# Weight splits one piece further ahead, in rings of five and four, in a two-layer encoder trunk

## The reference

```
h = rms_norm(x); proj = h @ w_in
gates, mla_in, dil_in, diff_in = split(proj)
o_mla  = latent attention (8 heads; q, k, v from normed latents @ w_uq, w_ukv; rope)
o_dil  = 3 dilated windows x 6 heads, mixed by their log-sum-exp; rope
o_diff = softmax(q1 k1) - lam softmax(q2 k2), 4 heads, rms_norm; rope
merged = g_mla*(o_mla @ w_branch_mla) + g_dil*(o_dil @ w_branch_dil) + g_diff*(o_diff @ w_branch_diff)
x = x + rms_norm(merged @ w_out)
h = rms_norm(x); u = conv3(h @ w_up); x = x + rms_norm((gelu(gate) * val) @ w_down)
```

## Time and profile before

| | us |
|---|---|
| median of 3 runs | 1046.75 (1046.65 to 1047.1) |
| the profiled execution | 1046.71 |
| its span | 1044.8 |
| TensorE busy | 1025.7 |
| VectorE busy | 656.4 |
| ScalarE busy | 586.6 |
| GpSimd busy | 121.7 |

### The profile page before, as it was taken

One profiled execution on the slowest core, in us unless ns is written; L12 is line 12 of the kernel. 1 busy time (PEld: TensorE's weight loads), 2 busy tenths in 40 slices (PEclk: granted clock), 3 DMA queues, 4 the chain that ended last, 5 costly groups with the idle time before them and its releaser, 6 DMA issues.

```text
span 1044.8 us, 15963 instructions
## 1 busy us (share of the span) xinstructions
PE 1025.7 (98%) x6332; PEld 918.9 (88%) x6332; DVE 656.4 (63%) x866; ACT 586.6 (56%) x843; POOL 121.7 (12%) x233
## 2 busy tenths in 40 slices
PE   8999999999999999999999999999999999999997
PEld 7889999888877999999898899998888789999996
DVE  5636556654585776776665355656556767676775
ACT  5666666556446645454475666565553466545453
POOL 3353114000000000000024321230000000000000
PEclk9999999999999999999999999999999999999999
DMA  8555445444453554546355544464445435554541
GB/s 253 178 180 158 128 128 190 142 143 161 142 190 112 202 201 162 203 160 220 103 191 163 165 129 124 149 201 161 138 148 178 163 139 179 185 201 163 201 161 41
DMA packets 106221, 170.79 MB, mean 163 GB/s; under 512 B 3377, under 2 KB 72804, under 8 KB 106148
## 3 DMA queue, kind: packets, MB, share of 16 engines
q1 hardware_dynamic: 104860, 166.88, 48.5%
q10 hardware_dynamic: 1208, 2.63, 0.7%
q0 software_dynamic: 80, 0.26, 0.1%
HBM read 168.72 MB, written 1.05 MB: 162 GB/s over the span
## 4 chain that ended last, share of the span: by engine, by line
PE 90%; DVE 4%; ACT 2%; DVEq 2%; issue 1%; POOL 0%; POOLq 0%; ACTq 0%
PE bank L1276 26%; PE bank L1278 26%; PE bank L1277 26%; PE bank L1566 2%; PE bank L1473 1%; PE bank L1494 1%; DVEq L1133 1%; PE bank L1559 1%; DVE merged L1134 1%; DVE hT_lo L1003 1%; PE bank L1482 1%; PE bank L1510 1%; PE bank L1255 1%; PE bank L1517 1%; PE bank L1556 1%
## 5 line engine op out<-in xcount | busy, mean ns | idle before, releaser
L982 DVE TENSOR_TENSOR w_lo<-w_raw,w_hi 128x2048 fp32r<-128x2048 f32 (+3 forms) x174 | 362.9, 2098 | 186.1 <-ACT w_hi L650 186.0
L650 ACT ACTIVATE w_hi<-w_raw 128x2048 fp32r<-128x2048 f32 (+3 forms) x174 | 302.4, 1752 | 49.8 <-PE bank L1278 49.2
L1276 PE MATMUL bank<-w_hi,hT_lo 128*128 128x512 f32 (+2 forms) x700 | 258.3, 369 | 0.7 <-DVE w_lo L982 0.6
L1278 PE MATMUL bank<-w_hi,hT_hi 128*128 128x512 f32 (+2 forms) x700 | 252.9, 361 | 0.0
L1277 PE MATMUL bank<-w_lo,hT_hi 128*128 128x512 f32 (+2 forms) x700 | 252.5, 361 | 0.0
L1276 PE MATMUL bank<-hT_hi,w_lo 128*128 128x256 f32 x704 | 199.9, 284 | 3.4 <-DVE hT_lo L1003 3.2
L1278 PE MATMUL bank<-hT_hi,w_hi 128*128 128x256 f32 x704 | 199.2, 283 | 0.0
L1277 PE MATMUL bank<-hT_lo,w_hi 128*128 128x256 f32 x704 | 199.2, 283 | 0.0
L1276 PEld LDWEIGHTS bank<-w_hi,hT_lo 128*128 128x128 f32 x700 | 131.5, 188 | 16.7 <-issue 2.0
L1278 PEld LDWEIGHTS bank<-w_hi,hT_hi 128*128 128x128 f32 x700 | 131.4, 188 | 14.1
L1277 PEld LDWEIGHTS bank<-w_lo,hT_hi 128*128 128x128 f32 x700 | 131.7, 188 | 13.0
(11 more groups left out here) (203 smaller groups left out, 1239.7 us busy)
## 6 DMA issues: line engine op xcount, KB each, us to landing
w_raw<-in_w_up_dram SPq DMA_DIRECT2D x44, 1024.0 KB, 4.9
w_raw<-in_w_in_dram SPq DMA_DIRECT2D x36, 1024.0 KB, 5.0
w_raw<-in_w_in_dram SPq DMA_DIRECT2D x36, 768.0 KB, 4.3
w_raw<-in_w_down_dram SPq DMA_DIRECT2D x22, 1024.0 KB, 5.3
w_raw<-in_w_out_dram SPq DMA_DIRECT2D x8, 1024.0 KB, 4.9
w_raw<-in_w_in_dram SPq DMA_DIRECT2D x8, 672.0 KB, 4.2
w_raw<-in_w_branch_mla_dram SPq DMA_DIRECT2D x4, 1024.0 KB, 4.9
w_raw<-in_w_branch_diff_dram SPq DMA_DIRECT2D x4, 1024.0 KB, 5.0
```

The costliest lines, as they stand in the source:

```text
L650: nc.scalar.activation(w_hi[:, n % RING, 0:nk * cols], raw[:, n % RING, 0:nk * cols], ACT.Copy).then_inc(hi_done, 1)
L982: V.tensor_tensor(w_lo[:, n % RING, s], raw[:, n % RING, s], w_hi[:, n % RING, s].bitcast(F32), ALU.subtract).then_inc(lo_done, 1)
L1276: PE.matmul(dst, lhs[1], rhs_hi, start=start, stop=False)
L1278: return PE.matmul(dst, lhs[0], rhs_hi, start=False, stop=stop)
```

## The change

`w_raw` becomes a ring of five, and `w_low`, a ring of five at the same address, takes the low parts: the subtraction reads the raw piece and writes its result over it. `w_hi` becomes a ring of four. Slots are counted through both layers. As a raw slot is now occupied until TensorE has used the piece, the load of piece g waits for the use of piece g-5 instead of the low split of g-3. The high part of piece g waits for the use of g-4. At step n the engines split piece n+3 instead of n+2; in step `pre` there is one more split (piece 2). Around `merged`, OUT0+1 on ScalarE comes two steps before the turn, OUT0+2 on both engines after it; after the MLP's turn UP0+2 is split instead of UP0+1. The other edits replace the counts.

```diff
-RING = 3
+HI_RING = 4
+LOW_RING = 5
@@ buffers
-        raw = sb("w_raw", [P, RING, 2048])
-        w_hi = sb("w_hi", [P, RING, 2048], F32R)
-        w_lo = sb("w_lo", [P, RING, 2048], F32R)
+        with ExitStack() as under:
+            raw = sb("w_raw", [P, LOW_RING, 2048], scope=under)
+        w_low = sb("w_low", [P, LOW_RING, 2048], F32R)
+        w_hi = sb("w_hi", [P, HI_RING, 2048], F32R)
@@ sync: the loads
-                    if l or n >= RING:
-                        sp.wait_ge(lo_done, l * NPIECE + (n + 1))
-                    if l == 0 and n == RING + 3:
+                    if l or n >= LOW_RING:
+                        sp.wait_ge(piece_used, l * NPIECE + (HI_RING + n + 1 - LOW_RING))
+                    if l == 0 and n == 6:
@@ scalar
             def split_hi(l, n):
-                nk, cols = PIECES[n][3:5]
-                act.wait_ge(raw_landed[n % RING], (l * (NPIECE // RING) + (n // RING + 1)) * 16)
+                g = l * NPIECE + n
+                act.wait_ge(raw_landed[g % LOW_RING], (g // LOW_RING + 1) * 16)
                 act.wait_ge(piece_used, l * NPIECE + (n + 1))
-                nc.scalar.activation(w_hi[:, n % RING, 0:nk * cols], raw[:, n % RING, 0:nk * cols], ACT.Copy).then_inc(hi_done, 1)
+                nc.scalar.activation(flat(w_hi, l, n), flat(raw, l, n), ACT.Copy).then_inc(hi_done, 1)
@@ scalar, steps
                         pre_attn(l)
+                        split_hi(l, 2)
...
+                        if step[1] == "merged":
+                            split_hi(l, OUT0 + 2)
                         if step[1] == "ffn":
-                            split_hi(l, UP0 + 1)
+                            split_hi(l, UP0 + 2)
...
-                        if n + 2 < NPIECE and n != UP0 - 1:
-                            split_hi(l, n + 2)
+                        if n + 3 < NPIECE and n not in (OUT0 - 1, UP0 - 1):
+                            split_hi(l, n + 3)
@@ vector
             def split_lo(l, n):
-                nk, cols = PIECES[n][3:5]
-                s = slice(0, nk * cols)
                 dve.wait_ge(hi_done, l * NPIECE + (n + 1))
-                V.tensor_tensor(w_lo[:, n % RING, s], raw[:, n % RING, s], w_hi[:, n % RING, s].bitcast(F32), ALU.subtract).then_inc(lo_done, 1)
+                V.tensor_tensor(flat(w_low, l, n), flat(raw, l, n), flat(w_hi, l, n).bitcast(F32), ALU.subtract).then_inc(lo_done, 1)
@@ vector, steps
                         pre_attn(l)
+                        split_lo(l, 2)
...
                         if step[1] == "ffn":
-                            split_lo(l, UP0 + 1)
+                            split_lo(l, UP0 + 2)
                         if step[1] == "merged":
                             split_lo(l, OUT0 + 1)
+                            split_lo(l, OUT0 + 2)
...
-                        if n + 2 < NPIECE and n not in (OUT0 - 1, UP0 - 1):
-                            split_lo(l, n + 2)
+                        if n + 3 < NPIECE and n not in (OUT0 - 2, OUT0 - 1, UP0 - 1):
+                            split_lo(l, n + 3)
```

More of the change, by code:

```diff
@@ L82 @@
 JOINED = [PIECES.index(("bdil", 0, 0, 2, 1024)), PIECES.index(("out", 1, 0, 4, 512))]
-assert NPIECE % RING == 0
 K_TOTAL = {"mla": 8, "diff": 8, "uq": 3, "ukv": 2, "dil": 8, "gate": 8, "bmla": 4, "bdiff": 4, "bdil": 3, "out": 8}
@@ L386, in build_trunk @@
         other_class = rope_b[:, 0:P]
-        raw_landed = [sem(f"raw_landed{i}") for i in range(RING)]
+        raw_landed = [sem(f"raw_landed{i}") for i in range(LOW_RING)]
         hi_done, lo_done, piece_used = sem("hi_done"), sem("lo_done"), sem("piece_used")
@@ L447, in weight_source, with flat, cut @@
             return view[l, :, k0:k0 + nk, c0:c0 + cols]
-        def cut(buf, n):
+        def flat(buf, l, n):
             nk, cols = PIECES[n][3:5]
-            return buf[:, n % RING, 0:nk * cols].rearrange("p (k n) -> p k n", k=nk)
+            ring = HI_RING if buf is w_hi else LOW_RING
+            return buf[:, (l * NPIECE + n) % ring, 0:nk * cols]
+        def cut(buf, l, n):
+            return flat(buf, l, n).rearrange("p (k n) -> p k n", k=PIECES[n][3])
         def own_order(cols):
@@ L475, in wait_tile @@
             if m in GROUP_END:
-                eng.wait_ge(piece_used, l * NPIECE + (RING + GROUP_END[m] + 1))
+                eng.wait_ge(piece_used, l * NPIECE + (HI_RING + GROUP_END[m] + 1))
             else:
@@ L510, in _ @@
                     sp.sem_inc(slot_claimed, 1)
-                    sp.dma_start(cut(raw, n), weight_source(l, *piece)).then_inc(raw_landed[n % RING], 16)
+                    sp.dma_start(cut(raw, l, n), weight_source(l, *piece)).then_inc(raw_landed[(l * NPIECE + n) % LOW_RING], 16)
             store_rows(sp, 0)
@@ L870, in _ @@
                             u, b = c // 2, c % 2
-                            act.wait_ge(piece_used, l * NPIECE + (RING + n + 1))
+                            act.wait_ge(piece_used, l * NPIECE + (HI_RING + n + 1))
                             if u >= 2:
@@ L886, in _ @@
                                 if u >= 2:
-                                    act.wait_ge(piece_used, l * NPIECE + (RING + PIECES.index(("down", u - 2, 0, 2, 1024)) + 1))
+                                    act.wait_ge(piece_used, l * NPIECE + (HI_RING + PIECES.index(("down", u - 2, 0, 2, 1024)) + 1))
                                 nc.scalar.activation(by_class2(g_hi[:, u % 2, :]), own_order2(conv[:, u % 2, 1, :]), ACT.Copy).then_inc(g_hi_done, 1)
@@ L899, in _ @@
             V = nc.vector
-            V.sem_inc(lo_done, RING)
             for started in (tile_emptied_dve, conv_done, o_emptied):
@@ L1246, in _ @@
             PE = nc.tensor
-            pe.sem_inc(piece_used, RING)
+            pe.sem_inc(piece_used, HI_RING)
             pe.wait_ge(ident_ready, 1)
@@ L1307, in use_first @@
             def use_first(n):
-                hi, lo = cut(w_hi, n), cut(w_lo, n)
+                hi, lo = cut(w_hi, 0, n), cut(w_low, 0, n)
                 k0, cols = PIECES[n][2], PIECES[n][4]
@@ L1319, in use_first @@
                         PE.matmul(bank[t][:, 0:cols], a_hi, hi[:, kk, :], start=False, stop=False)
-                    pe.wait_ge(lo_done, 1 + RING)
+                    pe.wait_ge(lo_done, 1)
                     for kk, t in left[0:4]:
@@ L1324, in use_first @@
                 else:
-                    pe.wait_ge(lo_done, n + 1 + RING)
+                    pe.wait_ge(lo_done, n + 1)
                 for kk, t in left:
@@ L1340, in use_piece @@
                 parts = [n - 1, n] if n - 1 in JOINED else [n]
-                hi, lo = cut(w_hi, n), cut(w_lo, n)
-                pe.wait_ge(lo_done, l * NPIECE + (n + 1 + RING))
+                hi, lo = cut(w_hi, l, n), cut(w_low, l, n)
+                pe.wait_ge(lo_done, l * NPIECE + (n + 1))
                 if kind == "up":
@@ L1384, in use_piece @@
                     for part in parts:
-                        hi, lo = cut(w_hi, part), cut(w_lo, part)
+                        hi, lo = cut(w_hi, l, part), cut(w_low, l, part)
                         p_k0, p_nk = PIECES[part][2:4]
```

## The result

The changed kernel takes **1050.68 us** (median of 6 executions, 1050.33 to 1052.6) against 1046.82 (6 executions, 1046.65 to 1047.43) of the kernel before, measured beside it: a ratio of 1.0040, 95% interval 1.0027 to 1.0053, or 3.9 us slower. The forecast was 1049.9, +3.2. The profiled execution took 1050.76 us with a span of 1048.9, 4.1 longer than before.

The account below looks back on a forecast made before the run. TensorE, busy 1025.7 of 1044.8 us, was taken as the bound. Start -0.1, merged turn -0.54 and rope +3.86 summed to +3.2 us, so 1049.9 us, range 1046.2 to 1051.0.

Parts of the forecast that it names:

- The bound: Whole kernel: TensorE busy 1025.7 of 1044.8 us, so the change wins only its idle time, 19 us at most, or adds waits.
- Part 1: Weight loads now follow TensorE's use of piece g-5; ScalarE may wait up to 2 us at short pieces; cost 0.
- Part 2: Low part written over the raw one by the same subtraction: no price either way.
- sign (4): Expected in the changed profile: no wait of TensorE or ScalarE above 1 us on a load.
- Part 3: Start: piece 4's low part earlier, tables and parameter copies later; net -0.1 us, between -0.6 and +1.0.
- Part 4: Turn of merged: a split leaves VectorE's merging run, which ends 0.27 us earlier per layer, 0.54 in both; bounds 0 and 1.9.
- Part 5: Alternating pieces 6 to 13: longer splits hold GpSimd's rope; 1.93 us lost per layer, 3.86 in both; bounds 0.7 and 6.
- rival A: Sixth rope's last operation starts before piece 12's split: 0.35 lost per layer, 1046.7; one layer only, 1048.3. Chance 0.25.
- The other stages: Gates, branches, MLP and turns: pieces of one size, no TensorE wait for weights, so moving splits changes nothing: 0.
- B: Only gains count because the rope chain catches up: 1045.6, or 1044.3 with the whole merged wait and start. Chance 0.08.
- C: Slower by more: parameter copies behind one more split (+1.0) or one more GpSimd hold per layer: 1051 to 1052.5. Chance 0.11.
- D: Loads bound: loads issued at the use of g-5 come late for TensorE, 1 us or more each, past 1060. Chance 0.02.

Follow-up runs that it names:

- experiment 1: Changed kernel with its rings, later loads and in-place low parts kept, but every split two pieces ahead again: 1045.24 us, ratio 0.9987.
- experiment 8: Changed kernel with GpSimd issuing the load of lam_rows before it waits for the tables instead of after: 1048.62 us, ratio 1.0018.
- experiment 6: Changed kernel with VectorE's parameter copies ahead of the scaling of mla_seq: 1048.68 us, ratio 1.0024.
- experiment 7: Changed kernel with the low split of piece 4 behind the angles again, as before: 1049.37 us, ratio 1.0026.
- experiment 2: Changed kernel with splits two pieces ahead only where big and small pieces alternate (steps 7 to 12): 1046.73 us, ratio 1.0002.
- experiment 5: Changed kernel with ScalarE, at step 7, copying the third tile to stage before making the high part of piece 10: 1046.41 us, ratio 0.9997.
- experiment 3: Changed kernel with VectorE beginning the low split of piece 12 only after the sixth tile is roped: 1048.15 us, ratio 1.0026.
- experiment 4: Changed kernel with the low split of piece 12 cut into four subtractions of 512 elements: 1047.28 us, ratio 1.0010.
- experiment 9: Changed kernel with splits two ahead where pieces alternate and parameter copies ahead of the mla_seq scaling: 1044.77 us, ratio 0.9982.
- experiment 10: Changed kernel with splits two ahead where pieces alternate and the lam_rows load issued before the wait for the tables: 1044.79 us, ratio 0.9982.

## Why the prediction was right or wrong, point by point

**The bound** was right: TensorE stays 98% busy, and the time moved with its waits, short ones inside rows included.

**Parts 1 and 2** (loads, in place, 0): right for the weights, and shown by experiment 1. The loads land in 5.0 us as before; ScalarE waits for one for 1.65 us at most (at 544.60). This is inside the 2 us foreseen, but over the 1 us that the prediction's sign (4) allowed; nobody behind it is late. What Part 1 did not ask is whether the earlier weight loads delay another load, that of `lam_rows`.

**Part 3** (start, -0.1) is the step that failed: its measured value is +1.06, a little past the upper bound of +1.0. The gain was right, and somewhat larger (0.95 instead of 0.6 us, of which 0.1 is an earlier landing of x in this execution). So was the mechanism, the parameter copies in place of the low part. What was mis-sized is the sentence that "tables, rope, roots and the scaling of `mla_seq` all come about 2.45 us later". Only the tables obeyed (2.26). The roots came 2.95 later (36.11 against 33.16), because the rope does not hang on the tables but on the landing of `lam_rows`, a load that GpSimd issues behind the tables and then drains: issued 2.26 later, it took 4.8 us instead of 4.2. The prediction does not mention it. Why it took longer stays open (experiment 8). The scaling then took 1.82 instead of 1.27 us, because the delay pushed it beside GpSimd's next rope, from 37.35 (0.55 lost), and the small split 1.47 instead of 1.36. 0.50 + 0.55 + 0.11 = 1.16, which is the distance from the forecast 39.9 to the measured 40.98 within 0.1. Experiments 6 and 8 each take the term back entirely, by different ends of the chain. The Trainium skill, page "SBUF — State Buffer", section "SBUF: two separate sides", warns that a DMA issued from GpSimd's queue can be starved while VectorE holds the shared ports, since GpSimd can't write the descriptors; the page says this of VectorE's two-port modes, and here it was float32 subtractions with two SBUF inputs. This case's traces do not bear it out for them: the load took 4.2 us where it was issued 0.77 us into a run of two such subtractions (the kernel before), and 4.2 us where it was issued 2.3 us ahead of the run (experiment 8).

The general fault is that Part 3 moved a chain as one block. A chain that crosses two engines which exclude each other, and waits for a load, changes its own length when it is moved.

**Part 4** (merged, -0.27 a layer): right, -0.29 and -0.30.

**Part 5** (rope and splits, +1.93 a layer): right in each step. The fourth rope is 0.36 and 0.35 late (0.35 forecast), the last operation of the sixth is held for 2.44 us, and each layer loses 1.98 and 1.97. The margin forecast as 0.05 was 0.03. That it held although the whole stage was shifted by 1.06 us was luck only in part: both ends of the race hang on the fourth rope, as the prediction argued, and experiments 6, 7 and 8, whose starts differ, show the same 3.0 us of waits on `stage` in two layers. Experiments 2 and 5 take the whole term away, by the pieces' alignment and by the copy at the root of it; experiments 3 and 4 take away its larger part, by the race's winner and by the length of the hold. Layer 1 repeated layer 0 within 0.01, so rival A's halfway case did not occur. Of the 115 ns of the Trainium skill ("SBUF — State Buffer", "SBUF: two separate sides"), which spoke for rival A: a held operation of 0.24 us ended 0.11 us after VectorE in experiment 8, the one of 0.32 that decides here 0.18 after, so the figure fits the short ones, and the measured rows decide.

**The other stages** (0): wrong by -0.36 between the layers. In the kernel before TensorE waits 0.36 us there for x_rows. GpSimd's roots end at 524.73 (524.19 + 0.54), and VectorE's work with them starts at 525.15, 0.42 later; in the changed kernel the roots end at 527.48 and the work starts at 527.54, 0.06 later. GpSimd's and VectorE's timelines, first of the kernel before, then of the changed one:

```profile
524.19 0.54 POOL L619 TENSOR_TENSOR roots<-mean_squares,minus_half 128x1 f32<-128x1 f32 x1 [2.47 <-DVE mean_squares L1094]
...
525.15 1.42 DVE L1114 SCALAR_TENSOR_TENSOR x_rows<-square_ffn,roots,x_rows 128x512 f32<-128x512 f32 x2 [0.45 <-POOL roots L619]
```

```profile
526.93 0.55 POOL L625 TENSOR_TENSOR roots<-mean_squares,minus_half 128x1 f32<-128x1 f32 x1 [2.47 <-DVE mean_squares L1100]
...
527.54 1.42 DVE L1120 SCALAR_TENSOR_TENSOR x_rows<-square_ffn,roots,x_rows 128x512 f32<-128x512 f32 x2
```

Experiment 3 had that wait too (0.4), experiments 1, 2 and 4 to 10 did not. No edit separates these groups, so its cause stays open; it need not be the change. That the total was missed by 0.8 us only is in part luck: this gain hides a third of the 1.16 us by which the start was wrong. Two readings of the earlier trace rows were wrong too, without a cost: the waits on `hT_lo` are six, not two (3.2 us before and after), and that view of the kernel before also has 0.9 us put down to a high part, at TensorE's first piece, which is 1.0 us in the changed kernel.

**The rivals.** A (the rope slips in) is out by 0.03 us; experiment 5 shows that it was near. B's prices of the gains alone, 1045.6 and 1044.3, enclose what remains once both losses are removed (1044.8). Of C only its first half came true, "the parameter copies fall behind", but by longer operations instead of one more split. D is out.

## What to carry to other kernels

Two engines that exclude each other turn a shift of a few hundredths of a microsecond into the length of the longest instruction of the other one, so when splits are moved to another step, write down which of them now meets which operation of the weaker engine, and cut the long instruction or let it wait where the race is close. When a step is put in front of a chain, don't move the chain as a block: walk it again operation by operation, look in it for DMAs that GpSimd issues and drains, and ask when they land. A lookahead that is good for pieces of one size can be bad where sizes alternate; it may be shortened for those few steps alone.

## What the runs showed of the hardware that was not expected

- A drain of GpSimd behind a DMA that it issued ended about 0.1 us after the landing of that DMA (33.72 against 33.6 in the changed kernel, 29.97 against 29.9 in experiment 8). The same 256 KB load took 4.2 to 6.1 us to land, and 4.2 both inside VectorE's run of subtractions and ahead of it.
- A GpSimd operation that waits can get in between two back-to-back VectorE operations: the multiply of 51.70, held by the first split, ends at 53.89, before the second split is over at 54.98, and the second multiply is held by that one (1.44).
- Small operations slow down too: four scalings of 384 elements took 1.82 us beside GpSimd's rope and 1.27 without it.
- Cutting a 2048-element subtraction into four cost VectorE 0.87 us and shortened the operation that decides from 2.44 to 0.84 us.
